# Gathering tokens for the experts with fp32 products instead of three bf16 pieces

## The reference

```python
def hierarchical_moe(h, router_group, router_expert, router_bias, expert_gate, expert_up, expert_down):
    tok = h.reshape(b * t, d)                      # 256 x 1024, RMS-normed
    group_prob = softmax(tok @ router_group)       # 4 groups
    group_p, group_idx = top_k(group_prob, 1)
    expert_logits = tok @ router_expert + router_bias      # 32 experts, 8 in a group
    top_logit, top_idx = top_k(in_group, 2)        # two experts of that group
    weights = softmax(top_logit) * group_p
    for e in range(32):
        y = (silu(tok @ expert_gate[e]) * (tok @ expert_up[e])) @ expert_down[e]
        out = out + combine[:, e:e + 1] * y
```

## Time and profile before

| | |
|---|---|
| median of 3 runs | 1043.15 us (1042.1 to 1043.86) |
| the profiled execution, first to last instruction (span) | 1041.0 us |
| between that span and the median | 2.15 us |
| TensorE busy, products / weight loads | 871.2 us / 629.5 us |
| VectorE / ScalarE / GpSimd busy | 353.5 / 219.6 / 28.2 us |
| mean granted TensorE clock | 0.945 of full |

### The profile page before, as it was taken

The page is one execution under the profiler, slowest core; times in us unless marked ns, Lnnn a source line. Parts: engine busy times, 40 slices in busy tenths (PEclk is TensorE's granted clock), DMA queues, the critical chain, the costliest instruction groups (busy, mean ns, idle before and its releaser), DMA issues.

```text
span 1041.0 us, 18150 instructions
## 1 busy us (share of the span) xinstructions
PE 871.2 (84%) x6932; PEld 629.5 (60%) x6933; DVE 353.5 (34%) x787; ACT 219.6 (21%) x416; POOL 28.2 (3%) x28
## 2 busy tenths in 40 slices
PE   5999999989588767798679999999895887879765
PEld 3877887978364434444358778879784543445332
DVE  1656634424621011111126565344346111112102
ACT  1233322322311010011103342133113111111111
POOL 2000000000300000000000000000003000000000
PEclk9999999999989898899879999999998998989888
DMA  9913012434459999989955120134334799899992
GB/s 343 353 47 102 1 41 82 162 122 162 168 229 419 420 420 421 421 326 421 401 190 182 40 82 1 42 122 162 113 150 168 302 421 421 339 423 419 420 421 109
DMA packets 48480, 249.47 MB, mean 240 GB/s; under 512 B 6096, under 2 KB 18560, under 8 KB 19344
## 3 DMA queue, kind: packets, MB, share of 16 engines
q1 hardware_dynamic: 47824, 246.91, 59.8%
q0 software_dynamic: 576, 1.43, 0.5%
HBM read 247.50 MB, written 1.05 MB: 239 GB/s over the span
## 4 chain that ended last, share of the span: by engine, by line
PE 49%; DMA 23%; DVE 13%; issue 7%; PEld 3%; ACT 2%; PEldq 1%; SPq 1%; DVEq 1%; POOLq 0%; ACTq 0%
DMA ring<-e_down 18%; PE ps L480 15%; PE ps L940 5%; PE ps L782 5%; PE ps L910 4%; PE ps L495 3%; PE ps L879 3%; DMA shared<-e_down 3%; DVE kq L1432 3%; DMA ring<-e_up 2%; DVE shared L1437 2%; PEld ps L910 1%; PE ps L679 1%; PE ps L634 1%; PE ps L951 1%
## 5 line engine op out<-in xcount | busy, mean ns | idle before, releaser
L480 PE MATMUL ps<-hT,ring 128*128 128x256 f32 x864 | 190.8, 380 | 0.0
L480 PEld LDWEIGHTS ps<-hT,ring 128*128 128x128 f32 x864 | 162.9, 190 | 25.4 <-DVEq L1249 2.0
L910 PE MATMUL ps<-ring,hT 128*32 128x256 f32 x1728 | 115.3, 426 | 42.8 <-DMA ring<-e_up 21.4
L910 PEld LDWEIGHTS ps<-ring,hT 128*32 128x32 f32 x1728 | 66.9, 122 | 91.1 <-issue 70.2
L879 PEld LDWEIGHTS ps<-kq 128*128 128x128 bf16 x960 | 64.9, 149 | 10.0 <-issue 7.4
L951 PE MATMUL ps<-hT,kq 128*128 128x512 f32 x144 | 66.1, 602 | 5.6 <-PE ps L940 5.6
L879 PE MATMUL ps<-kq 128*128 128x128 bf16 x960 | 67.7, 234 | 2.3 <-DVE kq L1617 2.3
L940 PE MATMUL ps<-ring,kq 128*32 128x512 f32 x448 | 52.6, 610 | 14.1 <-DMA ring<-e_down 10.1
L1617 DVE TENSOR_TENSOR kq<-shapes,sel 128x128 bf16<-128x128 f32 (+1 forms) x40 | 9.9, 288 | 158.1 <-PE ps L918 157.8
L782 PE MATMUL ps<-ring,xn 128*128 128x256 f32 x256 | 57.8, 381 | 0.0
L910 PE MATMUL ps<-shared,hT 128*32 128x256 f32 x576 | 40.0, 439 | 20.2 <-DMA shared<-e_up 18.7
(11 more groups left out here) (305 smaller groups left out, 1029.1 us busy)
## 6 DMA issues: line engine op xcount, KB each, us to landing
ring<-e_gate SPq DMA_DIRECT2D x48, 1024.0 KB, 21.7
ring<-e_up SPq DMA_DIRECT2D x48, 1024.0 KB, 11.0
ring<-e_down SPq DMA_DIRECT2D x48, 1024.0 KB, 23.7
ring<-w_mix SPq DMA_DIRECT2D x34, 1024.0 KB, 10.1
shared<-e_down SPq DMA_DIRECT2D x16, 1024.0 KB, 7.8
shared<-e_gate SPq DMA_DIRECT2D x16, 1024.0 KB, 18.8
shared<-e_up SPq DMA_DIRECT2D x16, 1024.0 KB, 26.5
ring<-w_mix SPq DMA_DIRECT2D x12, 512.0 KB, 7.1
```

The source lines that it names most:

```text
L480: mm = pe.matmul(bank[:, ct * T:(ct + 1) * T], w[:, k, ct * P:(ct + 1) * P], hT3[:, k, :], start=(k == 0), stop=(k == KD - 1))
L910: mm = pe.matmul(ps[32 * e:32 * e + 32, 5 + m, 0:DE], hq[:, k, 32 * e:32 * e + 32], slot[at[e]][:, k * DE:(k + 1) * DE], start=(k == 0), s ...
```

## The change

`gather` multiplies `xn` itself, in fp32, by an fp32 selection: 16 fp32 products instead of 48 bf16 ones. The splitting goes: two ScalarE roundings and two GpSimd subtractions, each in two halves, and their semaphores. TensorE's wait for the pieces becomes one for `xn`. `Psel` is fp32, so the tiles in `kq` move up; the final gain `gfin` lies in `kq` instead of the second half of `xn`, since `xn` is now read up to the last gather, and GpSimd issues its load and that of the next router weights earlier, having nothing ahead of them.

```diff
-        Psel = kq[:, 0:128].bitcast(BF16).rearrange("p (t s) -> p t s", t=TT)
-        Pwt = kq[:, 128:384].rearrange("p (t s) -> p t s", t=TT)
+        Psel = kq[:, 0:256].rearrange("p (t s) -> p t s", t=TT)
+        Pwt = kq[:, 256:512].rearrange("p (t s) -> p t s", t=TT)
...
-        part = [kq[:, 1408 + 1024 * i:1408 + 1024 * (i + 1)].bitcast(BF16).rearrange("p (t d) -> p t d", t=TT) for i in range(3)]
-        rest = hT[:, :].rearrange("p (t d) -> p t d", t=TT)
-        gfin = xn[:, D:2 * D]
+        gfin = kq[:, 1536:1536 + D]
...
                 pool.wait_ge(lgT_ready, 2)
-                for j in range(TT):
-                    pool.wait_ge(part_ready, j + 1)
-                    pool.tensor_tensor(rest[:, j, :], xn3[:, j, :], part[0][:, j, :], ALU.subtract).then_inc(rest_ready, 1)
-                for j in range(TT):
-                    pool.wait_ge(part_ready, TT + j + 1)
-                    pool.tensor_tensor(part[2][:, j, :], rest[:, j, :], part[1][:, j, :], ALU.subtract).then_inc(rest_ready, 1)
...
                             for j in range(TT):
-                                for i in range(3):
-                                    mm = pe.matmul(ps[:, 4 + 3 * half, kk * P:(kk + 1) * P], part[i][:, j, k:D:KD], Psel[:, j, :],
-                                                   start=(j == 0 and i == 0), stop=(j == TT - 1 and i == 2))
+                                mm = pe.matmul(ps[:, 4 + 3 * half, kk * P:(kk + 1) * P], xn3[:, j, k:D:KD], Psel[:, j, :],
+                                               start=(j == 0), stop=(j == TT - 1))
                         mm.then_inc(gath_full, 1)
 
-                pe.wait_ge(part_ready, 2 * TT)
-                pe.wait_ge(rest_ready, 2 * TT)
+                pe.wait_ge(xn_ready, 2 * TT)
...
                 rstd(rstd_ready)
-                for j in range(TT):
-                    act.wait_ge(xn_ready, 3 + j)
-                    act.activation(part[0][:, j, :], xn3[:, j, :], ACT.Copy).then_inc(part_ready, 1)
                 act.wait_ge(route_in, 1)
                 act.activation(rt[:, :, 24:28], rt[:, :, 20:24], ACT.Exp).then_inc(route_exp, 1)
-                for j in range(TT):
-                    act.wait_ge(rest_ready, j + 1)
-                    act.activation(part[1][:, j, :], rest[:, j, :], ACT.Copy).then_inc(part_ready, 1)
                 act.wait_ge(route_in, 2)
```

More of the change, by code:

```diff
@@ L245, in trunk @@
         ysb = hT[:, 1024:2048].rearrange("p (n s) -> p n s", n=2)
-        Psel = kq[:, 0:128].bitcast(BF16).rearrange("p (t s) -> p t s", t=TT)
-        Pwt = kq[:, 128:384].rearrange("p (t s) -> p t s", t=TT)
[L248 to L251, removed]
-        part = [kq[:, 1408 + 1024 * i:1408 + 1024 * (i + 1)].bitcast(BF16).rearrange("p (t d) -> p t d", t=TT) for i in range(3)]
-        rest = hT[:, :].rearrange("p (t d) -> p t d", t=TT)
-        gfin = xn[:, D:2 * D]
+        Psel = kq[:, 0:256].rearrange("p (t s) -> p t s", t=TT)
+        Pwt = kq[:, 256:512].rearrange("p (t s) -> p t s", t=TT)
+        PwT = kq[:, 512:768]
+        sg = kq[:, 768:1024]
+        hmid = kq[:, 1024:1280]
+        hmT = kq[:, 1280:1536].rearrange("p (f s) -> p f s", f=2)
+        gfin = kq[:, 1536:1536 + D]
         fin = shared[:, 0:TT * D].rearrange("p (t d) -> p t d", t=TT)
@@ L314, in trunk @@
         mask_ready = sem("mask_ready")
-        part_ready = sem("part_ready")
-        rest_ready = sem("rest_ready")
         acc_init = sem("acc_init")
```

## The result

The changed kernel takes 1050.66 us (median of 4 runs, 1050.52 to 1051.24), the kernel before 1043.01 us beside it (1042.1 to 1043.86): the ratio is 1.0075, 95% interval 1.0057 to 1.0092. It is slower by 7.65 us, where 8.6 us of gain was forecast. The time lies outside the range.

A forecast was written before the change was run, and what follows sets the result against it. Expert-stage transfers, started by each layer's first release, were taken to bound the kernel. Per layer 5.03 - 0.75 = 4.3 us, two layers 8.6 us of gain, gave 1034.5 us; the range was 1030 to 1038.

The forecast's parts named there:

- What bounds the kernel: Expert stages: transfers set the pace, the first release moves all behind it equally, TensorE's losses in rounds hide in DMA waits.
- step 4: 18 gathers inside the rounds: 0.5 to 0.8 us more each on TensorE, taken up by waits, costed at nothing.
- Step 1: Routing: without GpSimd's four subtractions, four held VectorE operations fall to 0.17 us each, 5.03 us less per layer.
- rival of the slow casts: Routing: casts are slow by nature, so only 2.65 us a layer is won; 1039.3 us, chance 0.07.
- Step 2: Routing: ScalarE's four roundings (1 us each) go, no gain of its own; earlier GpSimd loads cost nothing.
- step 5: Routing: `Psel` in fp32 takes the same two VectorE operations at one rate; no change.
- Step 3: Gather ahead of the rounds: 16 fp32 products take 6.1 us, 0.75 more than 5.34; bounds 3.7 and 7.2.
- third sign of being wrong: In the rounds: the waits for `e_down` behind the gathers vanish and TensorE sets the rounds; no size given.
- the other side: All gathers: strided fp32 weights load at half pace, 7.2 us a gather; 1048 us, chance 0.04.
- first rival: Gather ahead of the rounds: the clock stays up; 1030.9 us, or 1029.3 with 1.6 at the last down products; chance 0.14.
- "pause" rival: Second release in the expert stage does not move, so transfers run dry 4.3 us earlier; 1043 us, chance 0.03.
- the clock stays up: The first rival: TensorE keeps full clock at the gather ahead of the rounds, 6.1 us a layer won; chance 0.14.

The follow-up runs named there:

- Experiment 7: The kernel of experiment 1 with only the gather ahead of the rounds doing its 16 products twice; 1039.1 us, ratio 0.9967 to the kernel before.
- experiment 1: The changed kernel with xn stored block by block, so each gather product's 128 weights are adjacent; 1029.26 us, ratio 0.9864 to the kernel before.
- experiment 3: The kernel before without GpSimd's four subtractions, second and third pieces being zeros made by ScalarE; 1028.20 us, ratio 0.9856.
- experiment 4: The changed kernel with four GpSimd subtractions put back beside the routing, their result read by nobody; 1063.33 us, ratio 1.0196 to the kernel before.
- Experiment 2: The changed kernel with gather weights at four strides (adjacent, every second, fourth, eighth value), gathering wrong features; 1040.34 us, ratio 0.9968 to the kernel before.
- experiment 6: The kernel of experiment 1 with every gather inside a round doing its 16 products twice; 1053.01 us, ratio 1.0089 to the kernel before.
- experiment 9: The kernel of experiment 1 with TensorE repeating half of the copy of x while waiting for the routing; 1029.93 us, ratio 0.9895 to the kernel before.

## Why the prediction was wrong, step by step

Two terms failed, both from one wrong cost, the fp32 product with strided weights. The first gather was to cost 0.75 us more, and with the rank products it cost 1.9 to 2.1; the 18 gathers inside the rounds were put at nothing and cost 9.9 us in layer 0 and 4.8 in layer 1. The gain of 5.03 us a layer in the routing came as forecast.

**What bounds the kernel: right as to the first release.** Experiment 7 is the clean test: 3.6 us ahead of the first release move everything behind it by 3.6 us, 80 MB of transfers and the pause included. It is made from experiment 1's kernel; on the kernel before, experiment 3 agrees, with 5.6 and 6.2 us at the release and 0.2 us of change at most in the four stretches behind the releases. The second half, that what TensorE loses in a round is hidden, failed (step 4).

**Step 1, GpSimd's subtractions: right.** Four operations at 0.17 us in the changed kernel; the rank products 5.0 us earlier. Experiment 3 shows it with this part alone, experiment 4 by putting it back. The rule of the Trainium skill (SBUF — State Buffer, Who interferes with whom) is borne out by more than the rows of before: operations with two SBUF inputs, 0.17 us alone, took 1.81 and 1.70 us beside GpSimd's in experiment 4. It spoke against the rival of the slow casts, which is the second in the prediction's list and not the third.

**Step 2 and step 5: right.** ScalarE's roundings were worth nothing of themselves (experiment 3 has more of them), and the selection in fp32 takes 0.49 us for both halves, as before.

**Step 3, the gather ahead of the rounds: here it failed.** The prediction put an fp32 product with weights at a stride of 8 at 3.7 to 4.0 us a gather, "as those of line 832 have". Measured are 7.89 us, 0.247 a record, at full clock, and 7.92 with half of it at half clock. The row of line 832 was read rightly and was the wrong analogy: it is a transposition. In the changed kernel, in one profile, the same stride is loaded in 188 ns for transpositions of x

```profile
L821 PEld LDWEIGHTS ps<-shapes,x x32: 186/188/208, 266.5 to 790.4; 128*128 128x128 f32 x32
```

and in 335 ns for products of `xn`. (The transpositions of `xn` agree: 230 ns with the stride, 226 in experiment 1 without it.) Experiment 2 gives the pattern: for fp32 products the load takes 192 to 197 ns up to 8 bytes from value to value and 330 to 336 from 16 bytes on. The two bounds of the prediction, a contiguous product and a strided transposition, both lay below the truth. Each differed from the new operation in one feature, and the two features together made the price. Experiment 1 takes the stride away, and the gather falls to 3.84 us, inside the bounds.

**Step 4, "I cost it at nothing": failed with it.** The gather grew by 4.7 us, so a round takes some 24.4 us of TensorE instead of 19.6. The 18 gathers in the rounds add 85 us, and 14.7 of them show. The rest was taken up by waits of TensorE, above all for transfers, and these are more than the prediction looked at: in layer 0, behind the first release, TensorE waited 32.3 us in all for DMAs before and 10.5 now. From the first release to the gather of the two-round quad 138.3 us pass instead of 139.9, though the 4.6 us of the wait in experiment 6 are missing there. What is not covered stands around the stop of the transfers. From that gather to the second release it is 20.2 us for 16.1. Between the second release and the last down products of layer 0 there are three gathers, not one, 14.1 us of added work. Against them stood 1.48 us for `e_down` and this wait of the kernel before, which the prediction left out:

```profile
496.59 5.32 PE L910 MATMUL ps<-shared,hT 128*32 128x256 f32 x64 [4.29 <-DMA shared<-e_up]
```

Both are gone, and from 453.67 to 514.98 TensorE sets the pace: 61.3 us for two and a half rounds of 24.4, where five batches need 50. It is the prediction's third sign of being wrong. Experiment 6 shows that TensorE's time alone brings such a loss, though not its size.

**The rival "the other side" is what happened.** Its price was 1048 us, its condition a gather above 6.0 us; measured 7.9 and 1050.7, and experiment 2, at 5.9 us, comes out 0.3% under the kernel before. Its parts: 1.85 us lost at the first gather, measured 1.9 (5.03 less the 3.1 won); 5.6 a layer in the rounds, measured 9.9 and 4.8. That these come to 14.7 for its 11.2 is near, but by luck: it counted one gather at the layer's end where three stand, and a part of the waits. Its chance of 0.04 was too small: it rested on the one row of line 832, with its own doubt ("one record and not two") noted beside it and not paid for.

**The sum with the right pace.** Experiment 1 is the kernel of the forecast: 1029.3 and 1032.5 in two lots against 1034.5. Here the mis-sized term is the way to the first release: 5.4 and 5.2 us won, not 4.3, for two reasons. The first gather took 5.46 us, not 6.1; and the rank products ran at full clock, 0.8 us instead of 1.4, of which I had not thought. Another 1.6 us is won behind the last down products of the kernel, which take 3.64 us instead of 5.28 in every profile with an fp32 gather; the prediction had that only in its first rival. The "casts" rival and the "pause" rival are refuted (experiments 3 and 7); in the rival "the clock stays up" the clock fell, but later, inside the gather.

The Trainium skill's figure for a plain load (TensorE: Matmul & The Clock Gate, LDWEIGHTS), an estimated 107 ns, is near the adjacent case (0.115 us from one record's start to the next in experiment 1); the figure has no term for a stride, and it misses the strided case (0.24); its rule on fast loads (Weight-path perf modes) counts strided bf16 weights in, and the trace agrees only in part: 98 ns adjacent, 147 at every eighth value.

## What to carry to other kernels

Before fp32 operands replace bf16 ones, look at how far apart the weights lie: here 32 bytes from value to value doubled the price of an fp32 product, and a transposed layout, written by the operation that made the tile anyway, took it away for under 1 us. When no row shows the new operation, a price bounded by two rows that each differ in one feature is not bounded; the range has to reach to where both differences meet, and the rival there needs a real chance. Idle engines are not free to use: GpSimd's hidden work cost 5 us a layer by holding operations of 0.17 us on the path, and TensorE's waits inside a transfer-bound loop covered 70 of 85 us of added work, but not around the stop of the transfers. Waits have to be added up stretch by stretch, all of them and not only the one behind the changed work.

## What the runs showed of the hardware that was not expected

- Weight loads of fp32 products: 192 ns adjacent, 197 at 8 bytes, 330 at 16, 336 at 32 bytes from value to value; of transpositions at 32 bytes 188. Of bf16 products: 98 adjacent, 147 at 16 bytes. Why strided fp32 products fall to half pace and transpositions don't stays open.
- A gather bound by its loads takes the same time at either clock (7.92 us with a mean clock of 0.57 in its first 4 us, 7.89 at full clock).
- The granted clock fell to 0.50 inside the first gather although TensorE had done 1.9 us of added work and had idled ahead of it for 0.8 and 1.2 us only (experiment 9).
- A wait of 4.4 to 4.6 us without a releaser stands at the turn of the loop in layer 0 in the kernel before and in experiments 1, 6 and 7, and packets of the instruction queue go with it (experiment 6). Its cause is not shown.
- One version's runs, taken on two occasions, had medians of 1029.3 and 1032.5 us, each lot spreading over some 5 us.
